# Hybrid decoder step on one core: sample recurrence by pairs of heads, group-norm sums in threes, last down group by row chunks

## What is computed

```python
def step(S, inp):                       # RWKV-7, per head, S is 64 x 64
    r_t, w_t, k_t, v_t, a_t, b_t = inp
    sa = jnp.einsum('bhij,bhj->bhi', S, a_t)
    S = S * w_t[:, :, None, :] + sa[..., None] * b_t[:, :, None, :] + v_t[..., None] * k_t[:, :, None, :]
    return S, jnp.einsum('bhij,bhj->bhi', S, r_t)
...
mu = jnp.mean(y, axis=-1, keepdims=True)          # per head of 64
var = jnp.mean(jnp.square(y - mu), axis=-1, keepdims=True)
y = ((y - mu) * lax.rsqrt(var + GN_EPS)).reshape(Bn, T, A_WIDTH) * p['lnx_w'] + p['lnx_b']
out = (y + bonus) * g
...
x = x + hh @ p['w_down']                # hh has 2816 columns, x has 1024
y = rmsnorm(x, norm_final_g)            # the outputs y_prompt and y_sample
```

## Time and profile before

| | us |
|---|---|
| median of 3 runs | 1946.46 |
| lowest, highest | 1945.67, 1948.81 |
| profiled execution: device time | 1947.46 |
| profiled execution: span from first to last instruction | 1945.70 |
| PE busy | 1786.3 (92%) |
| VectorE (DVE) busy | 973.9 (50%) |
| ScalarE (ACT) busy | 484.3 (25%) |
| GpSimd (POOL) busy | 271.0 (14%) |

### The profile page before, as it was taken

One profiled execution on the slowest core, in us unless ns is written; L12 is line 12 of the kernel. 1 busy time (PEld: TensorE's weight loads), 2 busy tenths in 40 slices (PEclk: granted clock), 3 DMA queues, 4 the chain that ended last, 5 costly groups with the idle time before them and its releaser, 6 DMA issues. The chain is left out here.

```text
span 1945.7 us, 39461 instructions
## 1 busy us (share of the span) xinstructions
PE 1786.3 (92%) x17306; PEld 1601.8 (82%) x17306; DVE 973.9 (50%) x1730; ACT 484.3 (25%) x937; POOL 271.0 (14%) x357
## 2 busy tenths in 40 slices
PE   5999998997999758889979999999999999999996
PEld 4999994665666427888729999999999999999996
DVE  6233316775766385444344266445455455455455
ACT  6122113553222342222134321111111111111113
POOL 1000004324766030001011200000000000000000
PEclk8999998997999869999579999999999999999999
DMA  8211103102766200000042111110110111110203
GB/s 241 55 44 44 42 27 93 50 17 62 239 201 203 66 1 3 4 4 20 1 148 65 34 33 38 49 55 28 50 55 28 56 48 33 55 41 22 62 25 111
DMA packets 136613, 119.29 MB, mean 61 GB/s; under 512 B 16771, under 2 KB 123640, under 8 KB 136171
## 3 DMA queue, kind: packets, MB, share of 16 engines
q1 hardware_dynamic: 124507, 78.06, 13.6%
q0 software_dynamic: 11792, 38.17, 6.1%
q10 hardware_dynamic: 144, 0.52, 0.1%
HBM read 102.94 MB, written 11.44 MB: 59 GB/s over the span
## 5 line engine op out<-in xcount | busy, mean ns | idle before, releaser
L205 PE MATMUL bank<-normed2T_hi,w_hi 128*128 128x384 f32 (+1 forms) x1032 | 337.3, 327 | 0.0
L206 PE MATMUL bank<-normed2T_hi,w_lo 128*128 128x384 f32 (+1 forms) x1032 | 336.9, 326 | 0.0
L207 PE MATMUL bank<-normed2T_lo,w_hi 128*128 128x384 f32 (+1 forms) x1032 | 336.9, 326 | 0.0
L205 PEld LDWEIGHTS bank<-normed2T_hi,w_hi 128*128 128x128 f32 x1032 | 193.8, 188 | 1.6 <-issue 1.6
L207 PEld LDWEIGHTS bank<-normed2T_lo,w_hi 128*128 128x128 f32 x1032 | 193.8, 188 | 0.0
L206 PEld LDWEIGHTS bank<-normed2T_hi,w_lo 128*128 128x128 f32 x1032 | 193.8, 188 | 0.0
L205 PE MATMUL bank<-inner_hi,w_hi 128*128 128x384 f32 (+1 forms) x528 | 175.0, 331 | 10.2 <-DVE w_lo L494 7.1
L494 DVE TENSOR_TENSOR w_lo<-work,w_hi 128x1024 fp32r<-128x1024 f32 (+2 forms) x120 | 118.6, 989 | 130.6 <-ACT w_hi L489 129.4
L207 PE MATMUL bank<-inner_lo,w_hi 128*128 128x384 f32 (+1 forms) x528 | 174.7, 331 | 0.0
L206 PE MATMUL bank<-inner_hi,w_lo 128*128 128x384 f32 (+1 forms) x528 | 174.5, 330 | 0.0
L205 PE MATMUL bank<-normedT_hi,w_hi 128*128 128x384 f32 (+3 forms) x480 | 157.8, 329 | 5.6 <-DVE w_lo L494 5.6
(11 more groups left out here) (410 smaller groups left out, 3199.4 us busy)
## 6 DMA issues: line engine op xcount, KB each, us to landing
work<-in_w_up_dram SPq DMA_DIRECT2D x44, 512.0 KB, 3.9
work<-in_w_in_dram SPq DMA_DIRECT2D x19, 512.0 KB, 3.8
work<-in_w_down_dram SPq DMA_DIRECT2D x32, 256.0 KB, 2.7
residualT<-residual_spill SPq DMA_DIRECT2D x1, 4352.0 KB, 16.4
work<-in_x_prompt_dram SPq DMA_DIRECT2D x8, 512.0 KB, 5.6
residual_spill<-rwkv_streamsT SPq DMA_DIRECT2D x8, 512.0 KB, 4.4
work<-in_w_out_dram SPq DMA_DIRECT2D x8, 512.0 KB, 4.8
out_dram<-work SPq DMA_DIRECT2D x8, 512.0 KB, 2.7
```

Of the source, the lines that this page charges most:

```text
L205: pe.matmul(out, w[0], x[0], start=first, stop=False)
L206: pe.matmul(out, w[1], x[0], start=False, stop=False)
L207: return pe.matmul(out, w[0], x[1], start=False, stop=last)
```

## The change

It changes three stages and the order of the MLP's list.

1. *Sample part.* The 34 products become 19, by pairs of heads: PE issues the two heads of a pair alternately, into the two halves of one bank. The kinds run in the order 0, 2, 1, 3, 4. The 12 transposes of the states go into the solve, behind its third level (nat 0 and T4), and DVE's three copies behind levels four to six. The decay moves from the new state to its operands: DVE multiplies two sample slices of the streams by the decay at the start (`decay_stream`), and the old states after kind 1; after kind 4 only an add is left, for two heads at once. Spreading on DVE and POOL is for two heads at once, with three buffers each.
2. *Mixing.* One product per job sums the heads into 32 partitions of one bank; ACT scales the sums to negative means; the means are spread like the reciprocals, three chunks in a row into three banks; the sums of squares come in threes too. Every product of the first half now needs `heads_in`. Six buffers replace two and three.
3. *Last down group and final stage.* `GROUPS` becomes [4, 4, 4, 4, 4, 2]. The last group's weights come as two tiles of 2 x 512 columns, and its products run chunk by chunk. The final stage's barrier is gone: its transposes stand between the products of the second and third chunk, two tiles of banks instead of four; ACT and DVE follow.

```diff
+        PAIRS = [(what, m) for what in (0, 2, 1, 3, 4) for m in range(3)] + [("states", m) for m in range(3)]
+        PAIRS += [("prompt", 0)]
+        TURN_AT = 2
...
+                    if n >= 8:
+                        pair_taken(pe, PAIRS[n - 8])
+                    elif 4 <= n < 7:
+                        pe.wait_ge(st_cp, 3)
...
+                    elif what == 1:
+                        pair_taken(pe, (0, m))
+                        for h, r in two:
+                            pe.matmul(b[r, 0:NS], zs.wu[:, h, HD:P], ident[:, 0:NS], start=True, stop=False,
+                                      skip_group_check=True)
+                        for s in range(NB):
+                            cols = slice(TS * s, TS * s + TS)
+                            for h, r in two:
+                                last = pe.matmul(b[r, cols], s0[m][r, s * HD:(s + 1) * HD], wt[r, m, cols],
+                                                 start=False, stop=(s == NB - 1), skip_group_check=True)
...
+                    if n == TURN_AT:
+                        pe.wait_ge(s_sl, 128)
+                        for m in range(3):
+                            for q in range(4):
+                                last = pe.transpose(PS[4 + m][:, q * P:(q + 1) * P],
+                                                    SL[:, q // 2, q % 2, m * P:(m + 1) * P], ident)
+                            last.then_inc(st_t, 1)
...
+                def decay_stream(a):
+                    x = sT[:, 3 * a:3 * a + 3, SEQ:T].rearrange("p m (b t) -> p m b t", b=NB)
+                    dve.tensor_tensor(x, x, dc[:, :, nch:].unsqueeze(3).broadcast_to([P, 3, NB, TS]), ALU.mult
+                                      ).then_inc(sm_in, 1)
...
+                    dve.wait_ge(sm_mm, at_pair[1, m] + 1)
+                    dve.tensor_tensor(st, st, dc[:, m, nch:].unsqueeze(2).broadcast_to([P, NB, HD]), ALU.mult
+                                      ).then_inc(st_dec, 1)
+                for m in range(3):
+                    dve.wait_ge(sm_mm, at_pair[3, m] + 1)
+                    dve.tensor_tensor(um[m], both(pair_bank((3, m))[0:NS, :]), of_sequence, ALU.mult).then_inc(sm_dve, 1)
+                for m in range(3):
+                    dve.wait_ge(sm_mm, at_pair[4, m] + 1)
+                    dve.wait_ge(st_dec, m + 1)
+                    dve.tensor_tensor(s0[m], pair_bank((4, m)), s0[m], ALU.add).then_inc(sm_new, 1)
...
                 pe.wait_ge(s_hd, 16)
+                for m, c in jobs:
+                    last = pe.matmul(PS[0][32 * c:32 * c + 32, 0:384], heads_in[:, m, 0:32],
+                                     AR[:, m, 3 * c:3 * c + 3, 0], start=(m == 0), stop=(m == 2),
+                                     skip_group_check=True)
+                    if m == 2:
+                        last.then_inc(y_mean, 1)
+                pe.wait_ge(y_ms, 1)
+                spread_means(0)
+                spread_means(1)
                 pe.wait_ge(g_sig, 2)
+                gate_product(0)
+                variances(0)
+                spread_means(2)
+                gate_product(1)
+                variances(1)
+                gate_product(2)
+                variances(2)
                 pe.wait_ge(y_ri, 1)
+                for j in range(NJ):
+                    if j >= 3:
+                        pe.wait_ge(y_nrm, j - 2)
+                    spread(j, devs, y_bc)
+                    if j in (5, 8):
+                        for i in range(j - 2, j + 1):
+                            gate_product(i)
...
-        GROUPS = [4, 4, 4, 4, 3, 3]
+        GROUPS = [4, 4, 4, 4, 4, 2]
...
+        TILE_AT = {(c, m): 3 * (c - 1) + m // 2 - 1 for c in (1, 2) for m in (2, 4, 6)}
...
+                def turn_rows(i):
+                    pe.wait_ge(f_dn, DOWN0 + KD * (i // 3 + 1))
+                    if i >= 2:
+                        pe.wait_ge(e_y, 2 * (i - 1))
+                    for k in range(KD):
+                        last = pe.transpose(PS[4 + 2 * (i % 2) + k // 4][0:n, (k % 4) * P:(k % 4 + 1) * P],
+                                            xT[:, k, i * P:i * P + n], ident)
+                    last.then_inc(e_t, 1)
...
+                pe.wait_ge(f_hl, FT)
+                for c, (t0, n) in enumerate(CH):
+                    for m in range(KD):
+                        g = KD * c + m
+                        if c == 0:
+                            pe.wait_ge(w_lo, LAST + m // 4 + 1)
+                        if g >= 4:
+                            pe.wait_ge(f_dn, DOWN0 + g - 3)
+                        for k in range(halves_k):
+                            last = product(pe, PS[g % 4][:, 0:n], [w[:, k, cols] for w in wl[m // 4]],
+                                           [v[:, k, t0:t0 + n] for v in h2], k == 0, k == halves_k - 1)
+                        last.then_inc(f_mm, 1)
+                        if (c, m) == (1, 1):
+                            turn_history()
+                        if (c, m) in TILE_AT:
+                            turn_rows(TILE_AT[c, m])
+                for i in range(6, TT):
+                    turn_rows(i)
...
+                def add_down(c, m):
+                    t0, n = CH[c]
+                    g = KD * c + m
+                    dve.wait_ge(f_mm, 3 * LAST + g + 1)
+                    dve.tensor_tensor(xT[:, m, t0:t0 + n], PS[g % 4][:, 0:n], xT[:, m, t0:t0 + n], ALU.add
+                                      ).then_inc(f_dn, 1)
...
+                for c in (1, 2):
+                    for m in range(KD):
+                        add_down(c, m)
+                        if (c, m) in TILE_AT:
+                            total(TILE_AT[c, m])
+                        if (c, m - 1) in TILE_AT:
+                            scaled(TILE_AT[c, m - 1])
+                for i in range(6, TT):
+                    total(i)
+                    scaled(i)
```

More of the change, by code:

```diff
@@ new lines, in _ @@
+                for n, ops in enumerate(levels(i8)):
+                    for k in (1, 2):
+                        if (i8, "nat", k) in ops:
+                            pe.wait_ge(sm_in, k)
+                    products(pe, ops)
+                    if n == TURN_AT:
[5 more added lines that the diff above has]
+                            last.then_inc(st_t, 1)
@@ L2249, in build @@
         cw = Carve(loop_base)
-        ysq = [cw.take(384) for _ in range(2)]
-        yout = [cw.take(384) for _ in range(3)]
-        devs = cw.take(384)
+        ysq = [cw.take(384) for _ in range(6)]
+        yout = ysq
+        devs, means = cw.take(384), cw.take(384)
         heads_in = cw.take(480).rearrange("p (m c) -> p m c", m=3)
@@ L2413, in build @@
                 stream.append(("up", f))
-        stream += [("down", len(GROUPS) - 1, m) for m in range(KD)]
+        LAST = len(stream)
+        stream += [("last", i) for i in range(2)]
         NW = len(stream)
-        nth = {"gate": 0, "up": 0, "down": 0}
+        nth = {"gate": 0, "up": 0, "down": 0, "last": 0}
         order = []
```

454 lines of the change are left out of this document (214 added, 240 removed).

## The result

The changed kernel takes 1915.17 us (median of 4 runs, 1913.70 to 1917.94) where the kernel before takes 1946.31 in the same comparison (4 runs, 1945.67 to 1948.81): a ratio of 0.9839, 95% interval 0.9822 to 0.9856. The forecast was 1917.5 in a range of 1904 to 1933. The profiled execution took 1915.34, its span is 1913.2.

What follows compares the result with a forecast made beforehand. It took PE's own issue to bound sample part and mixing, and latency the final stage. Terms -15 (sample part), -5 (mixing) and -9 (last down group and final stage) sum to -29 from 1946.46: 1917.5, range 1904 to 1933.

Steps and rivals of the forecast that it cites:

- Solve with the turn inside: Sample part: state transposes inside the solve delay RT to 928.8, but kind 0 begins at 928.85 instead of 930.16, gaining 1.3.
- Kinds 0, 2, 1: Sample part: alternating small records cost 0.0325 at full clock, 0.056 at half; these kinds end at 941.1 instead of 956.20.
- rival price for this step: Sample part: alternating buys nothing at 8 columns, 192 records at 0.111, +10.6 and +2, kernel at 1930; chance 0.13.
- Kinds 3, 4 and the end: Sample part: kind 4 starts 2.05 after 941.1, takes 11.8 unchanged, the end loses 0.6; stage ends at 959.5, -15.0.
- Mixing: Mixing stage: both halves together save 5 us, bounds -11 and +1.5.
- First half: Mixing up to the root: waits 3.2 for c_heads, sums, spreads, centrings; root starts at 16.7 instead of 17.0, -0.3.
- I take the same: Mixing's first half: the clock rises some 4.2 us after the 18 sum records begin, as a profile row showed elsewhere.
- The rival for it: Mixing's first half: clock does not come back, root starts at 23.3, +6.3; kernel at 1924, chance 0.14.
- Second half: Mixing after root and reciprocal: spreads three side by side, 18.7 at half clock instead of 23.51, -4.8.
- Last down group and final stage: Kernel's end: last group starts at 1891.0, transposes hidden behind products, tiles 0 to 5 take 3.0 each, end 1936.7, -9.0.
- rival of one chain: Final stage: DVE's sum waits for its own tile's squares, rounds of 5.5 not 3.0, +15, kernel at 1932.5; chance 0.11.
- slower rival: Sample part: a bank's two halves exclude each other, 0.235 per small record, +36.5, kernel at 1954; chance 0.04.

Runs made afterwards that it cites:

- e5: Changed kernel with the small matmuls of kinds 1 and 2 going head after head instead of alternating between a pair's two heads: 1925.84 us, ratio 0.9877.
- e6: Changed kernel with the 12 state transposes and their copies put back behind the solve: 1912.54 us, ratio 0.9810.
- e12: Changed kernel with only mixing's gate products moved: first behind the sums, second between first and second spread groups, third behind the last variance product: 1911.48 us, ratio 0.9823.
- e4: Kernel before with only the group order 4, 4, 4, 4, 4, 2 and the old final stage: 1943.59 us, ratio 0.9981.
- e2: Kernel before with the mixing stage's change alone: 1943.74 us, ratio 0.9979.
- e8: Changed kernel with mixing's three early gate products moved behind the last variance product: 1913.38 us, ratio 0.9815.
- e9: Changed kernel with selector kept without a load, early gates behind the variances, state turn behind the solve, last three output tiles in freed banks: 1905.50 us.
- e10: e9 with gate products moved: first behind the sums, second between first and second spread groups, third behind the last variance product: 1902.18 us, ratio 0.9769.
- e11: e9 with 15 throwaway 128 x 128 products added between the narrow products of mixing's first half: 1910.21 us, ratio 0.9822, outputs wrong.

## Why the prediction was right, and where its steps were not

- **Solve with the turn inside.** Wrong in its reason and in two of its terms. It put PE's wait for the loads at 1.0 (0.3 here, 1.2 in e5) and gave the turn's new place a gain of 1.3. Kind 0 did come earlier, at 15.18 instead of 15.96 after the stage's start, but e6 has it at 14.52 with the turn in its old place. The gain is that kind 0 no longer waits for the copies. The decay multiplies were put under 0.4 each, in DVE's idle time; the first takes 2.03 and stands ahead of DVE's first work for the solve. In the nine other runs with this sample part PE therefore waits 1.3 for DVE, where it waited 0.7 before. In the changed kernel's profile this wait is 0.70 only because PE came late itself: it ran the solve's first products partly at half clock (0.60 from 909.66 to 911.66), and took 4.53 from its first product to the one that waits, against 3.60 in e5 and 2.98 before. POOL's spreads start beside the first multiply (5.75 for three); whether they held it up was not tested. The first two lines are the changed kernel's, the third e5's:

```profile
909.78 2.03 DVE L2220 TENSOR_TENSOR rwkv_streamsT<-rwkv_streamsT,small 128x192 f32<-128x192 f32 x1 [0.57 <-PEq L2064]
914.24 2.31 PE L1848 MATMUL bank<-residualT 64*64 64x64 f32 x72 [0.70 <-DVE residualT L2018]
...
919.33 2.31 PE L1848 MATMUL bank<-residualT 64*64 64x64 f32 x72 [1.32 <-DVE residualT L2018]
```

- **Kinds 0, 2, 1.** Right. I forecast 12.25 for them (by its own prices the third pair of kind 2 ends at 934.1 and not 934.5, which gives 11.9) and 12.97 was measured; the records stand at the price taken, a pair of kind 1 at 2.22 (931.15 to 933.37) for 2.2. The clock fell 17.5 after the stage's start instead of 19; in the other runs it fell between 17.7 and 20.1, in either order of the turn. The rival price for this step was too high: e5 shows 6.6 us for head after head, where I had 10.6 and 2 more.
- **Kinds 3, 4 and the end.** From the end of kind 1 to the end of the stage I forecast 18.4 and 17.2 was measured: kind 4 takes 10.4 (939.85 to 950.28) and not 11.8. Before, DVE's spreads for the last two heads stood behind its adds and decays (L2202 at 962.87 and 965.02); that they held up the last records was not tested. The shorter kind 4 makes up for kind 0 being 0.5 late and the clock's earlier fall, so the -15.0 came out to the tenth by luck, as errors that cancel. The scatter of the sample part between kernels of the same order is larger (43.5 to 45.3).
- **Mixing.** Near in size (-3.9 for -5, and -4.25 alone) by luck, wrong in both halves: they miss by +4.3 and -3.1. *First half*: forecast -0.3 with the clock back some 4 us behind the sums' start and staying; measured +4.0 (20.22 to 24.20). The clock came back when forecast and was lost at 965. The step that failed is "I take the same": it took one rise from a row and assumed that what follows would hold it. The rival for it (half clock throughout, +6.3) is the nearer. e12 shows the price: with the clock kept, the root comes at 15.2, ahead of the forecast's 16.7. *Second half*: forecast -4.8, measured -7.9 (23.51 to 15.62). The 18.7 (its terms add up to 18.5) assumed half clock to the end; after 9.0 us at 0.50 the clock came back, and the remaining 6.6 ran at 0.97.
- **Last down group and final stage.** Right in each piece: the last group starts 9.1 later behind the MLP's start (863.8 to 872.9, forecast 9.0), 45.5 us from there to the end (forecast 45.7), the first three turns 3.0 apart (1881.42, 1884.40, 1887.39) and the next three 2.6 (1891.96, 1894.60, 1897.23), where the rival of one chain needed 5.5. The order of groups: -3.0 alone in e4, forecast -2.9 (known to a microsecond or two), with all five `w_lo` waits at about 1.2.
- **The slower rival** fell at once: 0.032 a record, where it needed over 0.2.

## What to carry to other kernels

Issue small matmuls so that neighbours use different partition halves: at 64 x 64 weights and 8 columns it cut a record from 0.055 to 0.032 us at full clock and from 0.097 to 0.057 at half, in one bank. When narrow products replace wide ones, forecast the granted clock for each stretch and both its levels, and try where the remaining wide products stand: three of them moved shortened this stage by 5.5 to 7.0 us in one profiled execution, though the medians show only 2 us for the kernel. Look at the first instruction of each engine in a stage: a multiply put ahead of DVE's work for the solve cost PE 0.6 us where it was counted as covered. Sum a change by stages and by their starts; the span holds the scatter of parts that nobody touched, here up to 11.7 us.

## What the runs showed of the hardware that I had not expected

- The granted clock stood at 0.50 from 965.00 to 974.50 in the changed kernel, while PE was busy for all of these 9.50 us with variances, spreads and gate products; ahead of it PE did the spreads of the means. It stood at 0.97 from 988.20 on, where PE was busy 3.67 of 6.62.
- In mixing the clock stayed at 1.00, once back, for 3 to 5 us in the change, e2, e8 and e9, and for over 13 us in e10 and e12, which have two gate products ahead of the second group of spreads; in e5 and e6, with the change's mixing, it came back only 15 us after the stage's start. The rows are e2's as it was lost and e5's as it came back. Why two gate products did this and e11's 15 throwaway products did not is open; e10 and e12 are one profiled execution each.

```profile
979.28:980.28 1.00, 1.00 (x5) 0.73 (x4) 0.88 (x2) 0.91 (x2) 0.00 (x0) 0.61 1.13 328
...
982.49:983.49 1.00, 1.00 (x9) 0.31 (x6) 0.00 (x0) 0.00 (x0) 0.00 (x0) 0.98 1.32 557
```

- DVE's first multiply by the decay, 192 columns, took 2.03 in each of the ten profiled executions that have it, and POOL's first spread ran from the same time; the second took 0.66, and 1.60 in the changed kernel.
- The front, with the same instructions, took from 903.95 to 915.68 us. The cause was not looked for.
